# Four quadrants of the matrix array for row turning, decode products and 64-row sums, with ScalarE moving the second head pair back

## The chip, the cores and the metric

The kernel runs on one core of one Trainium2 chip. The metric is the device time of one execution in microseconds (us); less is better. Five engines work beside each other, each in the order of its own instruction list, and wait for each other by semaphores: TensorE (PE, and PEld for its loads of weights), VectorE (DVE), ScalarE (ACT), GpSimd (POOL) and SyncE (SP, which issues most DMAs).

## The reference

One inference step of a two-layer decoder. Each layer is a feed-forward block, a mixing block and another feed-forward block, all with residual adds. The mixing block projects the normed input once and splits the columns into four groups of heads: RWKV-7, RG-LRU, gated delta net (GDN) and gated linear attention (GLA).

```
x = x + 0.5 * _swiglu(_rmsnorm(x, norm_ffn1), ffn1_gate, ffn1_up, ffn1_down)
proj = _rmsnorm(x, norm_mix) @ w_in
o_rw, o_rg, o_gdn, o_gla = (the four groups, each 256 wide)
x = x + concatenate([o_rw, o_rg, o_gdn, o_gla]) @ w_out
x = x + 0.5 * _swiglu(_rmsnorm(x, norm_ffn2), ffn2_gate, ffn2_up, ffn2_down)
```

There are 256 prompt tokens of one sequence, worked in chunks of 64, and 8 x 8 decode tokens with given states: 320 tokens in all. Three groups have 4 heads of 64 values. In RWKV-7 and GDN the keys are scaled by the root of a sum of squares over the 64 rows of a head, and each decode sequence is multiplied with its own 64x64 state per head:

```
kk = _l2norm(_heads(k * rwkv_k_k, 64))            # x * rsqrt(sum(x*x) + 1e-12)
q = _l2norm(_heads(q, 64)) * 64 ** -0.5;  k = _l2norm(_heads(k, 64))
v_new = U - W @ S;  o = (q * eG) @ S + attn @ v_new
```

## The kernel before

Activations lie transposed: features on the 128 partitions, the 320 tokens (five chunks of 64, the fifth is the decode tokens) along the free axis. Four heads of 64 rows make two pairs p = 0, 1; within a pair head b = 0 is on partitions 0 to 63 and head b = 1 on 64 to 127 (`half[b]`). All operands with small matrices are of that form, so a product of one head has its operand on rows `half[b]` and its result, before the change, also on PSUM partitions `half[b]`: of the array's four 64x64 quadrants (row half, column half) only the two on the diagonal work.

Large products come from weight tiles of 128 x 1024. SP loads a tile (`raw`), ScalarE makes its high part (`split_hi`, L1124, 128x1024), VectorE the low part (`split_lo`, L1501), and TensorE multiplies in three terms (`three`, L477 to L479). A ring of four slots carries the tiles; ScalarE may write the high part of a unit only when the unit four before is used. From the fourteenth input tile on (`LATE`) only two places of `raw` are free, so a load waits until VectorE has made the low part of the unit two before.

In the mixing block the order of every engine is written out by hand. TensorE runs the 26 tiles of the input projection (each 24 matmuls of 128x320) and between them the small work: `lora`, `rw_sums` after tile 5, `rw_products` inside tile 9, `rw_rows` after tile 10, the steps of two 64x64 triangular inverses (`inverse_t` L774 and `inverse_y` L792, for g = 0 RWKV and g = 1 GDN), `gdn_sums` after tile 15, `gdn_products` (L631) after tile 19, `gdn_rows`, `gla_values`, and `decode_products` (L808) after tile 22 and in tile 23. Inverse steps already use all four quadrants: `inverse_unit(p, c, half[b ^ p])`. The same matmul in fp32 shows as two instructions in the trace. VectorE reads each tile out of PSUM (`evac`, L1572, L1573, L1582), which frees the bank for the tile after next, and does most of the elementwise work. ScalarE turns PSUM results into SBUF operands:

- `rw_rows`, `gdn_rows` and `gla_values` turn keys and values from columns to rows by a product with the identity (`to_rows`, L651); ScalarE copies each result (10 blocks of 64 columns, 128x640) out by one activation (L1285, L1287, L1289, L1348, L1350, L1356).
- `rw_sums` (L619) and `gdn_sums` (L666) sum squares over 64 rows with the 128x128 block-diagonal matrix of ones (`hones`); ScalarE takes Ln of each 128x320 result (L1268, L1319), then Exp.
- `decode_products(g)` writes 256 columns of bank 6 + g; ScalarE copies them out by one activation (`decode_out`, L1233). The stage after that needs them is `rg_gate`, which reuses the banks.
- `across` (L1219, L1220: two 64-partition copies that swap the halves) and `inverse_t` (L1211) on ScalarE serve the inverses. `gla_scale` (L1333, L1335) serves GLA.

Of the kernel before, what the change touches and what calls it, by code (L numbers as in the profile page):

```python
# [16 lines left out]
ACT = mybir.ActivationFunctionType  # L17
# [3 lines left out]
TOK = SEQ + DECB * DECT  # L21
GW, HD, NH, DK = 256, 64, 4, 32
CH = 64
# [101 lines left out]
    "hcen": 1, "yo": 1, "ysq0": 1, "ysq1": 1, "ysq2": 1, "cent_mm": 1, "cent_read": 1, "yrs": 3, "var_mm": 3, "VM": 4, "dec_mm": 3,  # L125
    "dec_decay": 3, "var_read": 3, "dec_add": 5, "sq_sum": 3,
}
V_STEPS, A_STEPS, G_STEPS = 102, 40, 14 + 3 * 6


class Signal:
# [43 lines left out]
def program(nc, xT, wts, par, cst, sin, mst, yT, sout, mout):  # L175
    with ExitStack() as ctx:
# [32 lines left out]
        ps = ctx.enter_context(nc.psum_tensor("ps", [128, 8, 512], F32))  # L209

        def A(u, n, pat=None, **kw):
            v = ar[:, u * TOK:u * TOK + n]
            return v.rearrange(pat, **kw) if pat else v
# [4 lines left out]
        def C(name, i=0, n=None):  # L218
            at, w = CST[name]
            return cs[:, at + i:at + i + (w if n is None else n)]  # L220
# [7 lines left out]
        rVt, kLt, bLt = (A(u, 640, CP, c=NC, p=2) for u in (18, 20, 22))  # L228
        gz, eG, kbe, qe = (A(u, 640, PT, p=2) for u in (24, 26, 28, 30))
        KQ = A(32, 1280, "q (c p k t) -> q c p k t", c=NC, p=2, k=2)  # L230
        bvt, gkdt = (A(u, 640, CP, c=NC, p=2) for u in (36, 38))
# [9 lines left out]
        ra, rsq, rtm = (A(u, 640, PT, p=2) for u in (47, 49, 40))  # L241
        gcp = A(73, 6 * CVP, PT, p=6)
        cq = A(52, 6 * TOK, PT, p=6)
        gsq = A(60, 4 * TOK, PT, p=4)
# [6 lines left out]
        lVt = A(75, 640, CP, c=NC, p=2)  # L251
# [23 lines left out]
        dec_out = [A(u, 256, "q (k p t) -> q k p t", k=2, p=2) for u in (42, 72)]  # L275
        nsq = A(49, 8 * TOK, PT, p=8)

        def mstate(name, p=2):
            at, n = MST[name]
            return ms[:, at:at + n].rearrange("q (p s v) -> q p s v", p=p, s=NSEQ)  # L280

        Mrw, Mgdn = mstate("rw"), mstate("gdn")
# [13 lines left out]
        half = [slice(0, 64), slice(64, 128)]  # L296
        I64 = [lev[half[b], 0, :] for b in range(2)]
# [29 lines left out]
        def banks(bank, runs, w=64):  # L327

            lo, hi = runs
            flat = ps[:, bank:bank + 3, :].rearrange("q b t -> q (b t)") if bank <= 5 else \  # L330
                ps[:, bank:8, :].rearrange("q b t -> q (b t)")
            return flat[:, lo * w:hi * w].rearrange("q (u t) -> q u t", u=hi - lo)
# [66 lines left out]
        def on(eng, layer, s, k=None):  # L399

            s = S[s] if isinstance(s, str) else s
            apart(eng, s, s.upto(layer, k)) if eng.engine in OWN_WAITS else eng.wait_ge(s.sem, s.upto(layer, k))
# [67 lines left out]
        def _(pe):  # L470
# [130 lines left out]
            def cht(v, c, p, b):  # L601
                return v[half[b], p, c * CH:(c + 1) * CH]


            def lora(layer):
                on(pe, layer, "lora_in")
                lo = P("lora", 0, 256)
                for rows, bank in ((slice(0, 32), 4), (slice(32, 64), 6), (slice(64, 128), 2)):
# [3 lines left out]
                        ins = pe.matmul(ps[:, bank + p, 0:TOK], lo[rows, p * 128:p * 128 + 128], xm[rows, 6, :], start=True, stop=True)  # L612
                    put(ins, "lora_mm")

            def rw_sums(layer):
                on(pe, layer, "sg")
                on(pe, layer, "kk_sq")
                for p in range(2):
                    ins = pe.matmul(ps[:, 4 + p, 0:TOK], C("hones"), rsq[:, p, :], start=True, stop=True)  # L619
                put(ins, "kk_sum")  # L620

            def rk_sums(layer):
# [24 lines left out]
            def to_rows(src, bank, name):  # L647

                def f(c, p, b):
                    u = c * 2 + p  # L650
                    return pe.matmul(ps[half[b], bank + u // 8, (u % 8) * 64:(u % 8) * 64 + 64], cht(src, c, p, b), I64[b],  # L651
                                     start=True, stop=True)
                put(each(f), name)

            def rw_rows(layer):
# [6 lines left out]
            def gdn_sums(layer):  # L662
                on(pe, layer, "gsq")
                on(pe, layer, "Gc")
                for k in range(4):
                    ins = pe.matmul(ps[:, 4 + k, 0:TOK], C("hones"), gsq[:, k, :], start=True, stop=True)  # L666
                put(ins, "gdn_sum")

            def gdn_decay(layer):
# [127 lines left out]
            def decode_products(layer, g):  # L797

                if g == 0:
                    on(pe, layer, "v_rows")  # L800
                    apart(pe, state_in, layer * 32 + 32)
                out = ps[:, 6 + g, 0:256].rearrange("q (k p t) -> q k p t", k=2, p=2)
                for q in range(DECB):
                    t = slice(q * DECT, q * DECT + DECT)
                    for p in range(2):
                        for b in range(2):
                            rhs = kkr[half[b], DEC, p, :, t] if g == 0 else kbe_qe[half[b], :, p, SEQ:][:, :, t]
                            ins = pe.matmul(out[half[b], :, p, t], (Mrw, Mgdn)[g][half[b], p, 1 + q, :], rhs, start=True, stop=True)  # L808
                put(ins, "R0_mm")

            def recurrences(layer):
# [306 lines left out]
        def _(act):  # L1118
# [58 lines left out]
            for layer in range(DEPTH):  # L1177
                st = Steps(act, a_step, layer, plain)

                def say(ins, name):  # L1180
                    return st(ins, S[name])
# [44 lines left out]
                def eye(g):  # L1226
                    if g == 0:
                        act.wait_ge(lo_ready.sem, layer * UNITS + IN0 + LATE)
                    say(act.activation(Y[g], lev[:, 0, :].unsqueeze(1).broadcast_to([128, 10, CH]), ACT.Copy), f"eye{g}")

                def decode_out(g):
                    on(act, layer, "R0_mm", g + 1)
                    say(act.activation(A(42 if g == 0 else 72, 256), ps[:, 6 + g, 0:256], ACT.Copy), "R0T")  # L1233

                ahead(1, 2)
                act.preload_act_table_set("sigmoid_and_others")
# [27 lines left out]
                act.wait_ge(S["prev"].sem, S["prev"].upto(layer))  # L1264
                say(act.activation(Pprev[:], sg[:], ACT.Exp, scale=-WDEC), "rw_P")
                act.wait_ge(S["kk_sum"].sem, S["kk_sum"].upto(layer))
                for p in range(2):
                    st(act.activation(rsq[:, p, :], ps[:, 4 + p, 0:TOK], ACT.Ln, bias=C("e12")))  # L1268
                st.settle()
                say(act.activation(rsq[:], rsq[:], ACT.Exp, scale=-0.5), "kk_rn")  # L1270
                on(act, layer, "gla_z")
                say(act.activation(ltm, ps[:, 6, 0:TOK], ACT.Abs, bias=P("gb")), "gla_ab")
# [9 lines left out]
                ahead(7, 8, 9)  # L1282
                eye(0)
                on(act, layer, "rw_rows_mm", 1)
                st(act.activation(rVt[:].rearrange("q c p t -> q (c p) t"), banks(2, (0, 10)), ACT.Copy))  # L1285
                on(act, layer, "rw_rows_mm", 2)
                st(act.activation(kLt[:].rearrange("q c p t -> q (c p) t"), banks(4, (0, 10)), ACT.Copy))  # L1287
                on(act, layer, "rw_rows_mm", 3)
                say(act.activation(bLt[:].rearrange("q c p t -> q (c p) t"), banks(6, (0, 10)), ACT.Copy), "rw_rows")  # L1289
                ahead(10, 11)  # L1290
                across(0, 1)
                inverse_t(0, 1)
# [22 lines left out]
                across(0, 3)  # L1315
                inverse_t(0, 3)
                act.wait_ge(S["gdn_sum"].sem, S["gdn_sum"].upto(layer))
                for k in range(4):
                    st(act.activation(gsq[:, k, :], ps[:, 4 + k, 0:TOK], ACT.Ln, bias=C("e12")))  # L1319
                st.settle()  # L1320
                say(act.activation(gsq[:], gsq[:], ACT.Exp, scale=-0.5), "gdn_rn")
                act.preload_act_table_set("exp_and_others")
                eye(1)
# [21 lines left out]
                inverse_t(0, 5)  # L1345
                ahead(20)
                on(act, layer, "gdn_rows_mm", 1)
                st(act.activation(bvt[:].rearrange("q c p t -> q (c p) t"), banks(4, (0, 10)), ACT.Copy))  # L1348
                on(act, layer, "gdn_rows_mm", 2)
                say(act.activation(gkdt[:].rearrange("q c p t -> q (c p) t"), banks(6, (0, 10)), ACT.Copy), "gdn_rows")  # L1350
                across(1, 1)
                inverse_t(1, 1)
                gla_scale(1)
                ahead(21)
                on(act, layer, "v_rows_mm")
                say(act.activation(lVt[:].rearrange("q c p t -> q (c p) t"), banks(6, (0, 10)), ACT.Copy), "v_rows")  # L1356
                gla_scale(2)
                across(1, 2)
                inverse_t(1, 2)
# [1073 lines left out]
```

## Time and profile before

| | |
|---|---|
| median of 3 runs | 1389.3 us (1388.21 to 1390.75) |
| the profiled execution's own time | 1388.47 us |
| its span in the trace | 1386.7 us |
| TensorE busy | 1353.0 us, 98% |
| VectorE busy | 862.9 us, 62% |
| ScalarE busy | 691.4 us, 50% |
| GpSimd busy | 75.4 us, 5% |
| mean granted TensorE clock | 0.997 |

Busy shares are means over stages with different limits. In the feed-forward stages TensorE streams without a pause. The two mixing blocks (about 254 to 435 us and 938 to 1119 us) are the only places that the change touches. A matmul is pipelined: its duration is longer than its distance to the next one, so rates are read from the length of a row that merges many.

### The profile page before, as it was taken

What the parts mean: (1) busy time and instruction counts of PE and PEld (TensorE: products, weight loads), DVE (VectorE), ACT (ScalarE), POOL (GpSimd) and SP (SyncE); (2) the same over time, 40 slices, a digit from 0 to 9 for tenths busy, and PEclk for the clock granted to TensorE, in tenths of its full rate; (3) what the DMA queues carried; (4) which work ended last, traced back from release to release, by engine and by line L of the source; (5) the groups of instructions that cost most, each with busy time, mean ns of one, the idle gap of its engine ahead of it and who ended that gap; (6) DMA issues with size and microseconds to landing.
All of it is one profiled execution on the core that took longest, in us unless ns stands there. A gap on an engine that the chain in (4) does not pass through costs nothing. (4 is left out here: it accounts for less than half of the span.)

```text
span 1386.7 us, 31381 instructions
## 1 busy us (share of the span) xinstructions
PE 1353.0 (98%) x12556; PEld 1308.9 (94%) x12556; DVE 862.9 (62%) x1329; ACT 691.4 (50%) x970; POOL 75.4 (5%) x109
## 2 busy tenths in 40 slices
PE   7999999999999999999999999999999999999997
PEld 7999999988888999999999999998888899999997
DVE  6656533897777765553475565358977767566433
ACT  7454433846455745443374453347455556454422
POOL 0000000200030100000010000010001301000000
PEclk9999999999999999999999999999999999999999
DMA  8544444313212544444454444433232135444441
GB/s 297 167 151 149 146 144 151 117 55 106 78 49 92 187 161 151 151 151 141 149 188 146 151 150 152 151 122 107 78 95 77 63 129 165 149 151 148 148 148 48
DMA packets 50765, 185.85 MB, mean 134 GB/s; under 512 B 5760, under 2 KB 6272, under 8 KB 50176
## 3 DMA queue, kind: packets, MB, share of 16 engines
q1 hardware_dynamic: 49104, 177.37, 39.4%
q10 hardware_dynamic: 1584, 7.35, 1.5%
q8 instruction: 60, 0.98, 0.3%
q14 instruction: 17, 0.14, 0.0%
HBM read 180.14 MB, written 4.56 MB: 133 GB/s over the span
## 5 line engine op out<-in xcount | busy, mean ns | idle before, releaser
L477 PE MATMUL ps<-xh,wh 128*128 128x320 f32 x1952 | 613.7, 314 | 12.7 <-DVE xl L1523 7.4
L1501 DVE TENSOR_TENSOR wl<-raw,wh 128x1024 fp32r<-128x1024 f32 x332 | 407.0, 1227 | 337.6 <-ACT wh L1124 337.2
L479 PE MATMUL ps<-xh,wl 128*128 128x320 f32 x1952 | 604.2, 310 | 0.0
L478 PE MATMUL ps<-xl,wh 128*128 128x320 f32 x1952 | 604.1, 310 | 0.0
L1124 ACT ACTIVATE wh<-raw 128x1024 fp32r<-128x1024 f32 x332 | 348.6, 1053 | 382.5 <-PE ps L479 371.5
L477 PEld LDWEIGHTS ps<-xh,wh 128*128 128x128 f32 x1952 | 367.5, 188 | 24.5 <-DVE wl L1501 7.8
L478 PEld LDWEIGHTS ps<-xl,wh 128*128 128x128 f32 x1952 | 367.7, 188 | 0.8
L479 PEld LDWEIGHTS ps<-xh,wl 128*128 128x128 f32 x1952 | 367.5, 188 | 0.0
L477 PE MATMUL ps<-hid_h,wh 128*128 (+1 forms) x704 | 217.9, 310 | 2.1 <-DVE hid_l L1548 2.1
L479 PE MATMUL ps<-hid_h,wl 128*128 (+1 forms) x704 | 217.5, 309 | 0.0
L478 PE MATMUL ps<-hid_l,wh 128*128 (+1 forms) x704 | 217.5, 309 | 0.0
L1165 ACT ACTIVATE gus<-gus 128x320 f32<-128x320 f32 x88 | 41.7, 473 | 189.7 <-DVE gus L1540 189.7
L477 PEld LDWEIGHTS ps<-hid_h,wh 128*128 128x128 f32 x704 | 132.1, 188 | 3.1 <-issue 3.1
L478 PEld LDWEIGHTS ps<-hid_l,wh 128*128 128x128 f32 x704 | 132.2, 188 | 0.0
L479 PEld LDWEIGHTS ps<-hid_h,wl 128*128 128x128 f32 x704 | 132.2, 188 | 0.0
L1540 DVE TENSOR_TENSOR gus<-ps,rstd 128x320 f32<-128x320 f32 x88 | 43.2, 491 | 101.4 <-PE ps L479 89.9
L2189 POOL TENSOR_TENSOR ar<-ar 128x320 f32<-128x320 f32 x35 | 31.7, 907 | 777.5 <-ACT ar L1147 773.4
L1165 ACT ACT_TABLE_LOAD x44 | 56.5, 1283 | 0.9
L1544 DVE TENSOR_TENSOR gus<-gus 128x320 f32<-128x320 f32 x88 | 43.4, 494 | 14.6 <-ACT gus L1165 2.6
L1548 DVE TENSOR_TENSOR hid_l<-gus,hid_h 128x320 f32 x88 | 42.6, 484 | 0.0
L1541 DVE TENSOR_TENSOR gus<-ps,rstd 128x320 f32<-128x320 f32 x88 | 42.3, 481 | 0.0
L1523 DVE SCALAR_TENSOR_TENSOR xl<-x,pr,xh 128x320 fp32r<-128x320 f32 x48 | 41.4, 898 | 0.1
(293 smaller groups left out, 974.5 us busy)
## 6 DMA issues: line engine op xcount, KB each, us to landing
raw<-wts SPq DMA_DIRECT2D x332, 512.0 KB, 3.5
ms<-mst ACTq DMA_DIRECT2D x2, 1440.0 KB, 9.2
mout<-ms ACTq DMA_DIRECT2D x2, 1440.0 KB, 7.2
x<-xT SPq DMA_DIRECT2D x4, 320.0 KB, 5.3
yT<-x SPq DMA_DIRECT2D x4, 320.0 KB, 2.2
cs<-cst SPq DMA_DIRECT2D x1, 652.0 KB, 9.0
pr<-par ACTq DMA_DIRECT2D x1, 429.0 KB, 4.1
pr<-par ACTq DMA_DIRECT2D x1, 425.0 KB, 5.2
```

The source lines that it names most:

```text
L477: pe.matmul(out, a, rh, start=start, stop=False)
L478: pe.matmul(out, a, rl, start=False, stop=False)
L479: return pe.matmul(out, b, rh, start=False, stop=stop)
L1124: act.activation(wh[:, s, :], raw_of(layer, n), ACT.Copy).then_inc(hi_ready.sem, 1)
L1165: act.activation(gus[:, m, :], gus[:, m, :], ACT.Silu).then_inc(sil_ready.sem, 1)
L1501: tt(wl[:, s, :], raw_of(layer, n), wh[:, s, :].bitcast(F32), ALU.subtract).then_inc(lo_ready.sem, 1)
L1523: stt(xl[:, k, :], x[:, k, :], P(name, k), xh[:, k, :].bitcast(F32), ALU.mult, ALU.subtract).then_inc(xl_ready.sem, 1)
L1540: tt(gus[:, m, :], ps[:, 2 * m, 0:TOK], rstd[:], ALU.mult).then_inc(gs_ready.sem, 1)
L1541: tt(gus[:, 2 + m, :], ps[:, 2 * m + 1, 0:TOK], rstd[:], ALU.mult).then_inc(gu_read.sem, 1)
L1544: tt(gus[:, m, :], gus[:, m, :], gus[:, 2 + m, :], ALU.mult).then_inc(act_ready.sem, 1)
L1548: tt(hid_l[:, at, :].rearrange("q a t -> q (a t)"), gus[:, m, :], hid_h[:, at, :].rearrange("q a t -> q (a t)").bitcast(F32), ALU.subtract ...
L2189: ins = gp.tensor_tensor(nsq[:, 0, :], nsq[:, 0, :], nsq[:, k, :], ALU.add)
```

## The change

Four things change, all in the mixing block.

1. `to_rows`: pair p = 1 writes to the opposite half (`half[b ^ p]`), each pair into a bank of its own (`bank + p`, 320 columns). The quadrants come in the order (0,0), (1,1), (0,1), (1,0). The number of matmuls is the same.
2. `rw_sums` and `gdn_sums`: each 128x128 product with the block-diagonal ones becomes two 64x64 products (`ones64`), for odd k in the crossed quadrants.
3. `decode_products`: pair 1 goes to the opposite half; both calls now use columns 0 to 127 of banks 6 and 7, so the second call first waits for ScalarE's copy of the first (`R0T`, 1).
4. ScalarE: what was one copy is now `home`: one activation of 128 partitions for pair 0, and two of 64 partitions that swap the halves for pair 1. `log_sums` does the same with Ln: one activation for even k, two for odd k. In all 19 more activations in each layer.

```diff
-V_STEPS, A_STEPS, G_STEPS = 102, 40, 14 + 3 * 6
+V_STEPS, A_STEPS, G_STEPS = 102, 59, 14 + 3 * 6
...
+            def ones64(b):
+                return C("hones")[half[b], 64 * b:64 * b + 64]
...
                 for p in range(2):
-                    ins = pe.matmul(ps[:, 4 + p, 0:TOK], C("hones"), rsq[:, p, :], start=True, stop=True)
+                    for b in range(2):
+                        ins = pe.matmul(ps[half[b ^ p], 4 + p, 0:TOK], ones64(b), rsq[half[b], p, :], start=True, stop=True)
...
                 def f(c, p, b):
-                    u = c * 2 + p
-                    return pe.matmul(ps[half[b], bank + u // 8, (u % 8) * 64:(u % 8) * 64 + 64], cht(src, c, p, b), I64[b],
-                                     start=True, stop=True)
+                    return pe.matmul(ps[half[b ^ p], bank + p, c * CH:c * CH + CH], cht(src, c, p, b), I64[b], start=True, stop=True)
...
                 for k in range(4):
-                    ins = pe.matmul(ps[:, 4 + k, 0:TOK], C("hones"), gsq[:, k, :], start=True, stop=True)
+                    for b in range(2):
+                        ins = pe.matmul(ps[half[b ^ k % 2], 4 + k, 0:TOK], ones64(b), gsq[half[b], k, :], start=True, stop=True)
...
+                else:
+                    on(pe, layer, "R0T", 1)
-                out = ps[:, 6 + g, 0:256].rearrange("q (k p t) -> q k p t", k=2, p=2)
+                out = ps[:, 6:8, 0:128].rearrange("q p (k t) -> q p k t", k=2)
...
-                            ins = pe.matmul(out[half[b], :, p, t], (Mrw, Mgdn)[g][half[b], p, 1 + q, :], rhs, start=True, stop=True)
+                            ins = pe.matmul(out[half[b ^ p], p, :, t], (Mrw, Mgdn)[g][half[b], p, 1 + q, :], rhs, start=True, stop=True)
...
+                def pieces(p):
+
+                    return ((half[0], half[1]), (half[1], half[0])) if p else ((slice(0, 128), slice(0, 128)),)
+
+                def home(dst, bank, name=None):
+
+                    for p in range(2):
+                        for to, at in pieces(p):
+                            d, n = dst[to, :, p, :], dst.shape[1]
+                            ins = act.activation(d, ps[at, bank + p, 0:n * CH].rearrange("q (c t) -> q c t", c=n), ACT.Copy)
+                            say(ins, name) if name and to is half[1] else st(ins)
+
+                def log_sums(dst, n):
+
+                    for k in range(n):
+                        for to, at in pieces(k % 2):
+                            st(act.activation(dst[to, k, :], ps[at, 4 + k, 0:TOK], ACT.Ln, bias=C("e12")[to]))
+                    st.settle()
...
-                    say(act.activation(A(42 if g == 0 else 72, 256), ps[:, 6 + g, 0:256], ACT.Copy), "R0T")
+                    home(dec_out[g], 6, "R0T")
...
-                for p in range(2):
-                    st(act.activation(rsq[:, p, :], ps[:, 4 + p, 0:TOK], ACT.Ln, bias=C("e12")))
-                st.settle()
+                log_sums(rsq, 2)
...
-                st(act.activation(rVt[:].rearrange("q c p t -> q (c p) t"), banks(2, (0, 10)), ACT.Copy))
+                home(rVt, 2)
...
-                for k in range(4):
-                    st(act.activation(gsq[:, k, :], ps[:, 4 + k, 0:TOK], ACT.Ln, bias=C("e12")))
-                st.settle()
+                log_sums(gsq, 4)
...
-                say(act.activation(lVt[:].rearrange("q c p t -> q (c p) t"), banks(6, (0, 10)), ACT.Copy), "v_rows")
+                home(lVt, 6, "v_rows")
```

ScalarE's list in the first layer, from the last inverse copy before GDN's sums (`raw<-ps`) through Ln, Exp, the table load and the identity copy to the high parts of the two next weight tiles. Before:

```order
145 L1211 ACTIVATE raw<-ps 128x2x16x8 [waits inv_mm0]
146 L1319 ACTIVATE ar<-ps,cs 128x320 [waits head_sums]
147 L1319 ACTIVATE ar<-ps,cs 128x320 x3
148 L1321 ACTIVATE ar<-ar 128x1280 [waits a_step]
149 L1322 ACT_TABLE_LOAD
150 L1229 ACTIVATE ar<-cs 128x640
151 L1124 ACTIVATE wh<-raw 128x1024 [waits unit_used,raw_in0]
```

And after the change (line numbers are those of the changed kernel):

```order
148 L1216 ACTIVATE raw<-ps 128x2x16x8 [waits inv_mm0]
149 L1252 ACTIVATE ar<-ps,cs 128x320 [waits head_sums]
150 L1252 ACTIVATE ar<-ps,cs 64x320 x2
151 L1252 ACTIVATE ar<-ps,cs 128x320
152 L1252 ACTIVATE ar<-ps,cs 64x320 x2
153 L1341 ACTIVATE ar<-ar 128x1280 [waits a_step]
154 L1342 ACT_TABLE_LOAD
155 L1234 ACTIVATE ar<-cs 128x640
156 L1129 ACTIVATE wh<-raw 128x1024 [waits unit_used,raw_in0]
```

Four Ln activations have become six; nothing else moved. The second place on ScalarE is the copy of GLA's values, between a weight tile's high part and the scale of GLA's second level, ahead of the inverse copy (`chain<-ps`) for which TensorE waits. Before:

```order
168 L1124 ACTIVATE wh<-raw 128x1024 [waits unit_used,raw_in1]
169 L1356 ACTIVATE ar<-ps 128x640 [waits v_rows_mm]
170 L1333 ACTIVATE ar<-ar 128x320 [waits lD]
171 L1335 ACTIVATE ar<-ar 128x320 [waits a_step]
172 L1219 ACTIVATE ar<-ar 64x320 [waits XY1]
173 L1220 ACTIVATE ar<-ar 64x320
174 L1211 ACTIVATE chain<-ps 128x80x4 [waits inv_mm1]
```

After:

```order
175 L1129 ACTIVATE wh<-raw 128x1024 [waits unit_used,raw_in1]
176 L1245 ACTIVATE ar<-ps 128x5x64 [waits v_rows_mm]
177 L1245 ACTIVATE ar<-ps 64x5x64 x2
178 L1353 ACTIVATE ar<-ar 128x320 [waits lD]
179 L1355 ACTIVATE ar<-ar 128x320 [waits a_step]
180 L1224 ACTIVATE ar<-ar 64x320 [waits XY1]
181 L1225 ACTIVATE ar<-ar 64x320
182 L1216 ACTIVATE chain<-ps 128x80x4 [waits inv_mm1]
```

One copy has become three. On TensorE the order stays as it was; in the decode products of the second group (g = 1, between the inverse step and GLA's first level) one wait is new. Before:

```order
1017 L774 MATMUL ps<-chain,ar 64x64 [waits XY1]
1018 L774 MATMUL ps<-chain,ar 64x64 x15
1019 L808 MATMUL ps<-ar,ms 64x2x8 x32
1020 L724 MATMUL ps<-ar 64x64 [waits gdn_rows]
1021 L724 MATMUL ps<-ar 64x64 x19
```

After:

```order
1017 L777 MATMUL ps<-chain,ar 64x64 [waits XY1]
1018 L777 MATMUL ps<-chain,ar 64x64 x15
1019 L813 MATMUL ps<-ar,ms 64x2x8 [waits R0T]
1020 L813 MATMUL ps<-ar,ms 64x2x8 x31
1021 L727 MATMUL ps<-ar 64x64 [waits gdn_rows]
1022 L727 MATMUL ps<-ar 64x64 x19
```

## Rows read from the trace of the kernel before

**Rows 1.** The page's first part: busy time by engine.

```profile
PE 1353.0 (98%) x12556; PEld 1308.9 (94%) x12556; DVE 862.9 (62%) x1329; ACT 691.4 (50%) x970; POOL 75.4 (5%) x109
```

**Rows 2.** Busy time in stretches; columns: length, then engines, clock, DMA share, GB/s.

```profile
295.00:330.00 35.00, 33.03 (x472) 29.79 (x470) 32.78 (x62) 18.08 (x26) 1.47 (x2) 0.95 0.25 77
...
349.00:370.00 21.00, 20.68 (x448) 19.07 (x445) 20.52 (x41) 10.87 (x21) 2.99 (x5) 1.00 0.27 87
370.00:377.00 7.00, 7.00 (x176) 6.59 (x176) 2.14 (x3) 2.66 (x5) 0.00 (x0) 1.00 0.26 84
```

**Rows 3.** TensorE in order of time, 295 to 373 us: start, length, count.

```profile
295.28 3.71 PE L651 MATMUL ps<-cs,ar 64*64 64x64 f32 x120
...
302.64 0.81 PE L774 MATMUL ps<-raw,ar 64*64 64x64 f32 x40
...
327.82 2.42 PE L666 MATMUL ps<-ar,cs 128*128 128x320 f32 x8
...
370.80 2.04 PE L808 MATMUL ps<-ar,ms 64*64 64x16 f32 x64
```

**Rows 4.** What TensorE waited for, 255 to 430 us: total, times, longest.

```profile
PE ps L477 <- DVE ar L1573: 1.6, 1, 1.6
PE ps L690 <- DVE ar L1641: 1.1, 1, 1.1
PE ps L774 <- DVE raw L1879: 0.7, 1, 0.7
...
PE ps L631 <- DVE ar L1720: 0.5, 1, 0.5
```

**Rows 5.** TensorE in the second layer, after tile 16.

```profile
1017.14 0.27 PE L792 MATMUL ps<-raw 64*64 64x64 f32 x2 [1.30 <-ACT raw L1211]
```

**Rows 6.** ScalarE in order of time, 328 to 345 us; in brackets the idle time before.

```profile
328.98 0.63 ACT L1223 ACTIVATE ar<-ar 128x512 f32<-128x512 f32 x1 [0.56 <-DVE ar L1658]
...
333.29 0.36 ACT L1211 ACTIVATE raw<-ps 128x256 f32<-128x256 f32 x1
333.67 1.78 ACT L1319 ACTIVATE ar<-ps,cs 128x320 f32<-128x320 f32 x4
...
338.72 1.99 ACT L1124 ACTIVATE wh<-raw 128x1024 fp32r<-128x1024 f32 x2
...
344.53 1.06 ACT L1124 ACTIVATE wh<-raw 128x1024 fp32r<-128x1024 f32 x1 [0.41 <-DMA raw<-wts]
```

**Rows 7.** VectorE in order of time, 339 to 348 us.

```profile
339.79 1.23 DVE L1501 TENSOR_TENSOR wl<-raw,wh 128x1024 fp32r<-128x1024 f32 x1 [4.08 <-ACT wh L1124]
...
345.62 1.22 DVE L1501 TENSOR_TENSOR wl<-raw,wh 128x1024 fp32r<-128x1024 f32 x1 [1.13 <-ACT wh L1124]
...
347.56 0.81 DVE L1720 TENSOR_TENSOR ar<-ar,ps 128x640 f32<-128x640 f32 x1
```

**Rows 8.** ScalarE's copies: a pair of 128x320 out of PSUM, and the crossing pieces.

```profile
309.51 0.74 ACT L1295 ACTIVATE ar<-ps 128x320 f32<-128x320 f32 x2
...
359.33 0.47 ACT L1219 ACTIVATE ar<-ar 64x320 f32<-64x320 f32 x1
359.83 0.47 ACT L1220 ACTIVATE ar<-ar 64x320 f32<-64x320 f32 x1
360.20 0.68 ACT L1211 ACTIVATE chain<-ps 128x640 f32<-128x640 f32 x1
```

**Rows 9.** ScalarE, 365 to 368 us.

```profile
365.15 0.70 ACT L1356 ACTIVATE ar<-ps 128x640 f32<-128x640 f32 x1
365.76 0.47 ACT L1333 ACTIVATE ar<-ar 128x320 f32<-128x320 f32 x1
...
367.63 0.41 ACT L1211 ACTIVATE chain<-ps 128x320 f32<-128x320 f32 x1
```

**Rows 10.** TensorE at the inverse step after tile 22's first half.

```profile
368.10 0.40 PE L792 MATMUL ps<-ar,chain 64*64 64x64 f32 x12 [0.32 <-ACT chain L1211]
```

**Rows 11.** The same six microseconds in layer one and layer two.

```profile
316.00:322.00 6.00, 5.17 (x40) 5.19 (x41) 5.72 (x11) 5.07 (x7) 1.47 (x2) 0.72 0.35 97
1000.00:1006.00 6.00, 5.57 (x87) 5.32 (x88) 5.68 (x12) 4.92 (x7) 1.47 (x2) 1.00 0.35 113
```

More of the change, by code:

```diff
@@ L1284, in _ @@
                 on(act, layer, "rw_rows_mm", 1)
-                st(act.activation(rVt[:].rearrange("q c p t -> q (c p) t"), banks(2, (0, 10)), ACT.Copy))
+                home(rVt, 2)
                 on(act, layer, "rw_rows_mm", 2)
-                st(act.activation(kLt[:].rearrange("q c p t -> q (c p) t"), banks(4, (0, 10)), ACT.Copy))
+                home(kLt, 4)
                 on(act, layer, "rw_rows_mm", 3)
-                say(act.activation(bLt[:].rearrange("q c p t -> q (c p) t"), banks(6, (0, 10)), ACT.Copy), "rw_rows")
+                home(bLt, 6, "rw_rows")
                 ahead(10, 11)
@@ L1347, in _ @@
                 on(act, layer, "gdn_rows_mm", 1)
-                st(act.activation(bvt[:].rearrange("q c p t -> q (c p) t"), banks(4, (0, 10)), ACT.Copy))
+                home(bvt, 4)
                 on(act, layer, "gdn_rows_mm", 2)
-                say(act.activation(gkdt[:].rearrange("q c p t -> q (c p) t"), banks(6, (0, 10)), ACT.Copy), "gdn_rows")
+                home(gkdt, 6, "gdn_rows")
                 across(1, 1)
```

## The prediction

> **What bounds the kernel now.** I read the busy shares first. TensorE is busy for 98% of the span [rows 1], which invites the conclusion that every nanosecond taken from it is gained. The windows of the mixing block correct that: from 295 to 330 us TensorE is busy for 33.0 of 35 us, but VectorE for 32.8 of 35 as well, and from 349 to 370 the two have 20.7 and 20.5 of 21. Only from 370 on is TensorE alone full (7.0 of 7 us, VectorE 2.1) [rows 2]. So in most of the stretch two engines run neck and neck, and the waits must say who leads. TensorE's waits are small but they lie all along: for VectorE's evacuation ahead of tile 9 (1.6 us), its transpose (0.7) and its bonus product (1.1) at 314 to 317 us, and its value product (0.5) ahead of L631 [rows 4]. In layer two it also waits 1.30 us for ScalarE's inverse copy after tile 16 [rows 5]. Wherever such a wait stands, time that TensorE saved ahead of it only makes the wait longer. I therefore go from one of these meeting points to the next and ask at each whether the engine that TensorE meets has moved.
>
> **The rates.** An inverse step in all four quadrants takes 0.81 us for 40 instructions; take off 0.22 for the tail of the last one, and it is 15.1 ns from one to the next. Row turning on the diagonal takes 3.71 us for 120, which is 29.3 ns, and the decode products 2.04 us for 64, 29.0 ns [rows 3]. If the other two quadrants work as they do in the inverse step, one turn of 40 instructions falls by 39 x 14.2 ns = 0.55 us, a decode call by 63 x 13.9 ns = 0.88 us. The wide sums take 2.42 us for 8 instructions, 0.284 us each after the tail [rows 3]; four quadrants need half the time, so GDN's sums save 1.14 us and RWKV's, half as many, 0.57.
>
> TensorE thus saves per layer: 6 turns x 0.55 = 3.3, two decode calls 1.76, sums 1.71, together 6.8 us. What of it is on the path?
>
> **To tile 9.** RWKV's sums (0.57) are followed by the 1.6 us wait for VectorE [rows 4], whose work up to there needs nothing from the sums until ScalarE's Exp, and that has 2 us to spare. Gain 0. ScalarE's third Ln (below, 0.5 us) fits into the same room. Cost 0.
>
> **Row turning of RWKV to tile 16.** Three turns save 1.7 us at 297 us. The following inverse step needs ScalarE's halves swap, which waits for VectorE's GLA decay; VectorE has no idle time between 297 and 332 us in its timeline. The waits of 0.7 and 1.1 us at 314 to 317 us are for VectorE too [rows 4]. Gain 0. ScalarE's three copies become nine, some 1.8 us more; it ends near 300.3 instead of 299.7, and TensorE needs them only after tile 11, at 301. Cost 0.
>
> **GDN's sums, where the change costs.** They save 1.14 us at 330 us, but the next thing after tile 16 is an inverse step that starts at 333.70, right after ScalarE's copy ended at 333.65; that copy hangs on a chain which VectorE's convolution released at 328.98 [rows 6]. In layer two TensorE waits 1.30 us there already [rows 5]. Gain 0. Then ScalarE is the leader: Ln from 333.67, Exp, a table load, the identity, and the high part of a weight tile at 338.72 [rows 6], for which VectorE has idled 4.08 us; its low part lets the DMA for the unit two on start, the next high part waits 0.41 us for that DMA, VectorE 1.13 us for this high part, and then come the products that end with L1720, for which TensorE waits 0.5 us [rows 4, 6, 7]. There is no slack in this chain. Two more Ln at (1.78 - 0.55) / 3 = 0.41 us each are 0.82 us. A crossing piece is followed by the next after 0.50 us instead of the 0.37 us of a plain piece [rows 8], which happens twice: 0.26 more. Bounds 0.8 and 1.2; I take 1.0, since the rows for crossing pieces read SBUF and not PSUM. The lower end below that is nothing, if pieces of 64 partitions overlap; I keep 0 for a rival. So L631 starts 1.0 us later.
>
> The Trainium skill, TensorEngine Tiling (Array Packing), "PSUM Bottleneck", says that packing the array speeds up TensorE but not the way out of PSUM, which may then become the limit. The rows above bear that out for ScalarE here; by it the sign of this step is a loss, which the sum already has.
>
> **GDN's turns and GLA's.** TensorE would save 1.1 us in GDN's two turns, but ScalarE takes the weight tile's high part after tile 20 before it can copy, so it starts no earlier; six pieces at 0.37 to 0.50 us instead of two copies (0.61 us from one start to the next [rows 9]) end about 1.3 us late, the inverse step follows 1.3 late. VectorE, already 1.0 late from above and without a gap, hides the rest. GLA's turn saves 0.55 into that same lateness. Its copy stands 0.61 us ahead of the next activation [rows 9]; three pieces at 0.37 + 0.50 + 0.37 = 1.24 us [rows 8] are 0.63 more (bounds 0.5 and 0.9), and the inverse copy at 367.63 comes directly behind it. TensorE waits 0.32 us for exactly this copy [rows 10]. So the inverse step at 368.10 starts 1.0 + 0.6 = 1.6 us late. Every turn's gain is gone.
>
> **Decode.** From 370 to 377 us TensorE has no idle time [rows 2], so the two calls count in full: minus 1.76 us. The new wait for R0T hides behind tile 23's first half (2.0 us) and an inverse step (0.7): ScalarE has been waiting for the products and needs some 0.6 us for three pieces of 128 columns. Behind the waiting instruction are GLA's first level and half a tile; if the cover were gone the wait would cost 0.6.
>
> **Sum.** Per layer +1.0 +0.6 -1.76 = -0.16 us, both layers -0.3 us. The profiled execution took 1388.47 us for a span of 1386.7; -0.3 gives 1388.2. The median of the runs is 0.8 above that execution, so on it I forecast 1389.0 us. With the bounds of the two ScalarE terms (0.8 to 1.2, 0.5 to 0.9) the forecast alone reaches from -0.9 to +0.7 us, and with the spread of the three runs from 1387.5 to 1390.5.
>
> **Rivals.**
> - TensorE alone decides. Then all 6.8 us per layer count and the time is 1375.7. For it speaks the 98%; against it every wait in rows 4 and 5. Chance 0.04.
> - ScalarE's pieces cost nothing at its two tight places, for instance because 64-partition pieces overlap. Then only the decode gain is left: -3.5 us, 1385.8. With some of the turns' gain 1384. Against it: the crossing pieces now take 0.50 us [rows 8]. Chance 0.15.
> - The decode products gain nothing, and the kernel gets slower. Their instructions of 16 columns go at 29.0 ns like those of 64 columns [rows 3], so streaming does not set their pace; if it is something that both column halves share, such as the loading of weights through a row half, four quadrants bring nothing. It decides as soon as a call keeps more than 1.9 of its 2.04 us. Then +1.6 per layer stays: +3.2, 1392.5. Against it: the inverse step loads a new weight for every instruction too and goes at 15.1 ns. Chance 0.10.
> - The clock falls. From 316 to 322 us it is 0.72 of full (in part at the lower of its two levels, 1.2 GHz), behind TensorE's waits of 0.7 and 1.1 us; at the same place in layer two it stays 1.00 [rows 11]. That cost 0.28 x 6 = 1.7 us, unseen since VectorE led. The change adds idle time of 1 to 2.5 us ahead of three meeting points. A fall between 349 and 370 us would hit where little slack is: up to 1.7 us per layer, 1392.4. Chance 0.07.
>
> The skill's same page, "Gotcha 1: PSUM Pressure", says that different row tiles cannot use one PSUM bank at the same time. Here two row halves write one bank both before and after, and the inverse step does so at 15.1 ns. If the rule governed, the decode products would gain nothing, which is the third rival; the trace disagrees.
>
> **How the numbers follow.** The forecast has 0.64. What a measurement of this kernel can tell from no change is about 0.2%, 2.8 us. Faster than that: the first two rivals, 0.19. Slower: most of the last two, just beyond the bound, 0.16. The rest, 0.65, is the same. The range holds 8 in 10 from 1385.2, which takes in most of the second rival, to 1392.2.
>
> **What would show it.** L774-like rates in the new turns and decode calls (0.81 and about 1.16 us); TensorE waiting longer for VectorE at 314 to 317 us, about 1.1 us more after tile 16, and over 1 us ahead of L631; six Ln in 2.6 to 3.0 us; L631 about 1.0 us later than now after the common start of the layer; the inverse step of rows 10 about 1.6 us late; the start of GLA's first level within 0.5 us of where it was. Wrong would be a shortened stretch between tile 9 and L631, or a decode call that is still near 2 us.

## The result and the profile after

The change made the kernel slightly slower: 1391.49 us median of 20 runs against 1389.03, ratio 1.0016 with a 95% interval of 1.0009 to 1.0023. One execution of each kernel took 4.6 ms; the ratio leaves these two out. The forecast was 1389.0 us and no change. The time lies inside the range of 1385.2 to 1392.2, and 2.5 us is within the 0.2% that the text called the same, but the loss is clear of the interval and the sign of the forecast sum (-0.3 us) was wrong. The profiled execution took 1391.6 us for a span of 1389.8.

The busy line answers [rows 1]: TensorE has 9 us less to do and the kernel is later.

```profile
PE 1343.9 (97%) x12580; PEld 1298.3 (93%) x12580; DVE 862.1 (62%) x1329; ACT 703.6 (51%) x1008; POOL 75.3 (5%) x109
```

TensorE in order of time, first layer (start, length, count, idle before and who ended it). These answer [rows 3, 5, 10].

```profile
294.88 1.98 PE L654 MATMUL ps<-cs,ar 64*64 64x64 f32 x120
309.29 0.27 PE L795 MATMUL ps<-raw 64*64 64x64 f32 x2 [1.54 <-ACT raw L1216]
327.35 1.26 PE L669 MATMUL ps<-ar,cs 64*64 64x320 f32 x16
333.33 0.27 PE L795 MATMUL ps<-raw 64*64 64x64 f32 x2 [1.00 <-ACT raw L1216]
349.59 2.40 PE L635 MATMUL ps<-ar 64*64 64x128 f32 x40 [1.91 <-DVE ar L1740]
362.42 0.80 PE L795 MATMUL ps<-ar,chain 64*64 64x64 f32 x38 [1.40 <-ACT chain L1216]
369.94 0.81 PE L795 MATMUL ps<-ar,chain 64*64 64x64 f32 x40 [1.07 <-ACT chain L1216]
372.63 1.12 PE L813 MATMUL ps<-ar,ms 64*64 64x16 f32 x64
```

The three RWKV turns take 1.98 us instead of 3.71, GDN's sums 1.26 instead of 2.42, a decode call 1.12 instead of 2.04: the quadrants do what they should. The saved time went into waits: new ones of 1.54 us where the row is at 309 and of 1.00 us after tile 16, 1.91 us at L635 (it was 0.5 in [rows 4]), 1.40 and 1.07 at the inverse steps (the latter 0.32 in [rows 10]). The waits for VectorE ahead of tile 9 and at 314 to 317 us stayed at 1.6, 0.7 and 1.1 us. The prediction had looked for longer waits at 314 to 317 us; what the RWKV turns saved went into the wait for ScalarE's inverse copy at 309 instead.

ScalarE in the two tight places, and the first three Ln one by one; these answer [rows 6, 9].

```profile
333.30 3.28 ACT L1252 ACTIVATE ar<-ps,cs 128x320 f32<-128x320 f32 x6
...
333.30 0.53 ACT L1252 ACTIVATE ar<-ps,cs 128x320 f32<-128x320 f32 x1
333.85 0.53 ACT L1252 ACTIVATE ar<-ps,cs 64x320 f32<-64x320 f32 x1
334.41 0.52 ACT L1252 ACTIVATE ar<-ps,cs 64x320 f32<-64x320 f32 x1
...
339.84 1.99 ACT L1129 ACTIVATE wh<-raw 128x1024 fp32r<-128x1024 f32 x2
...
366.25 1.33 ACT L1245 ACTIVATE ar<-ps 128x320 f32<-128x320 f32 x3
367.60 0.47 ACT L1353 ACTIVATE ar<-ar 128x320 f32<-128x320 f32 x1
...
369.47 0.41 ACT L1216 ACTIVATE chain<-ps 128x320 f32<-128x320 f32 x1
```

The Ln group takes 3.28 us instead of 1.78: +1.50. A Ln of 64 partitions lasts as long as one of 128 (0.53 us), and none starts before the one ahead of it has ended (0.55 us from start to start), while the four of before overlapped (0.41). GLA's copy takes 1.35 us up to the next activation instead of 0.61: +0.74.

The path through both mixing blocks, measured from the layer's first LoRA product (261.80 and 945.39 us before, 261.38 and 945.53 after; worked out from the rows of both traces):

| us from the layer's first LoRA product | layer 1 before | after | layer 2 before | after |
|---|---|---|---|---|
| L631 (after: L635) starts | 86.72 | 88.21 | 86.58 | 89.79 |
| inverse step of [rows 10] starts | 106.30 | 108.56 | 106.15 | 110.13 |
| first decode call starts | 109.00 | 111.25 | 108.84 | 112.82 |
| GLA's first level starts | 115.37 | 115.78 | 115.21 | 117.35 |
| head centering (L992, L997) starts | 162.20 | 162.77 | 161.61 | 164.61 |

From the end of the first block to the start of the second, and behind the second, nothing differs by more than 0.1 us. The sum is 0.57 + 3.00 = 3.6 us, less 0.4 that this execution began its first layer earlier: 3.1 us, the difference of the spans. Up to GLA's first level, layer one is as the forecast had it but for sizes. Two more things come in, both larger in layer two. One is TensorE's clock (windows of the changed kernel; the column before the last two is the granted clock):

```profile
316.00:322.00 6.00, 5.55 (x43) 5.57 (x44) 5.68 (x12) 4.26 (x6) 1.47 (x2) 0.72 0.34 111
1000.00:1008.00 8.00, 7.43 (x48) 7.26 (x48) 6.19 (x12) 4.58 (x6) 1.47 (x2) 0.57 0.39 132
```

In layer one the clock falls as before [rows 11], 0.28 x 6 = 1.7 us of full speed, and VectorE hides it. In layer two it falls for twice that, 0.43 x 8 = 3.4 us, where before it stayed at 1.00. Tile 14 then ends so late that VectorE has to wait for it, and L635 comes 3.2 instead of 1.5 us late:

```profile
1008.08 0.49 DVE L1600 SCALAR_TENSOR_TENSOR ar<-ps,rstd 128x320 f32<-128x320 f32 x1 [1.57 <-PE ps L479]
```

The other is a stop in the recurrences, of which the profile shows no cause:

```profile
1094.36 0.21 PE L824 MATMUL ps<-ar 64*64 64x64 f32 x1 [0.67 <-issue]
```

In all it is 1.0 us in two stops in this kernel (0.31 us in layer one, 0.67 in layer two), and none in the kernel before. So the 3.6 us of the profiled execution are 0.8 from the sizes on the path, 1.7 from the long fall and 1.0 from the stops.

How often the long fall comes can be read from the mean granted clock of every execution. Seven of the 19 executions of the changed kernel read 0.995 or less, and they took 1391.4 to 1393.7 us; the other twelve took 1390.0 to 1391.9 with a median of 1390.8, 0.6 below the median of all 19. Of the 79 executions of the kernel before that were timed beside the experiments, five read 0.995 (1390.1 to 1391.2 us) and none less; from 0.996 to 0.999 a lower reading did not go with a longer time. So the long fall adds some 0.6 us to the median of the changed kernel; this is an estimate, since only the profiled executions show where the clock fell.

### The profile page after: what moved, and what is told of

It reads as the page before. It is cut to its first block and busy times, and to the rows that moved or that the text cites. A ratio compares the mean times of both kernels' runs of the same rounds, so it can differ in the third digit from the quotient of the medians.

```text
span 1389.8 us, 31467 instructions
## 1 busy us (share of the span) xinstructions
PE 1343.9 (97%) x12580; PEld 1298.3 (93%) x12580; DVE 862.1 (62%) x1329; ACT 703.6 (51%) x1008; POOL 75.3 (5%) x109
```

## The experiments

All are timed beside the kernel before, whose median in the three batches was 1388.93, 1389.3 and 1389.2 us; each ratio is to its own batch. The two kernels with the identity later have five executions each, GDN's sums alone nine, the others eleven. GLA's first level is read from one profiled execution, in us after the layer's first LoRA product; that product itself starts between 261.4 and 262.6 us in the thirteen profiled executions, so medians less than about 1 us apart say little about the mixing blocks. Theory 1: ScalarE's pieces do not overlap, and their two tight places (+1.5, +0.7 us per layer) outweigh the two decode calls (-1.84). Theory 2: falls of the clock make the loss. Theory 3: the stops come from where the instruction stream stands (in the first expectation "theory 3" is the third rival of the prediction).

| kernel | median us | ratio to before, 95% | GLA's first level, layer 1 / 2 |
|---|---|---|---|
| before | 1389.0 | 1 | 115.37 / 115.21 |
| the change | 1391.5 | 1.0016 (1.0009 to 1.0023) | 115.78 / 117.35 |
| decode alone | 1385.2 | 0.9975 (0.9966 to 0.9984) | 113.41 / 113.32 |
| GDN's sums alone | 1392.7 | 1.0025 (1.0015 to 1.0035) | 116.92 / 118.40 |
| turns alone | 1390.6 | 1.0010 (1.0001 to 1.0019) | 116.07 / 115.97 |
| change, GDN's sums as before | 1386.5 | 0.9983 (0.9974 to 0.9992) | 114.19 / 114.27 |
| change, turns and sums uncrossed | 1390.9 | 1.0015 (1.0006 to 1.0024) | 115.95 / 117.58 |
| change, filled after tile 13 | 1391.0 | 1.0017 (1.0007 to 1.0026) | 115.55 / 115.58 |
| change, all longer waits filled | 1390.5 | 1.0009 (1.0000 to 1.0018) | 115.59 / 115.63 |
| before, filled after tile 13 | 1389.0 | 0.9998 (0.9989 to 1.0007) | 115.13 / 115.20 |
| GDN's sums as before, 8 instructions more | 1387.7 | 0.9990 (0.9981 to 0.9999) | 114.37 / 114.40 |
| decode, identity later | 1384.5 | 0.9963 (0.9950 to 0.9977) | 112.84 / 114.58 |
| decode, identity later, filled | 1383.9 | 0.9961 (0.9948 to 0.9975) | 112.81 / 112.82 |

**Decode alone.** The kernel before with only the two edits in `decode_products` and `home` in `decode_out`.

> The kernel before with the decode products alone changed (four quadrants, one copy into three pieces). Theory 1 (what decides is ScalarE: its pieces do not overlap each other, each costs its full duration, which makes the two tight ScalarE places 1.5 and 0.7 us later per layer, against 1.84 us that the two decode calls give per layer): both tight places are untouched, so the gain stands alone, 2 x 1.84 = 3.7 us below before, ratio 0.9973, and the first level of GLA starts about 1.8 us earlier in each layer. Theory 2 (the loss of the full change comes from TensorE's clock, which falls at tile 14 after more idle time): no idle time is added ahead of tile 14, so the clock is as before and the gain stands too. Theory 3 (the decode products gain nothing): ratio 1.000.

Measured 3.7 us below before, as theory 1 has it; the interval is 1.2 us to either side, so the match to the tenth is luck. The third rival, that 16-column products gain nothing, is out:

```profile
370.69 1.12 PE L810 MATMUL ps<-ar,ms 64*64 64x16 f32 x64
```

**GDN's sums, taken out and put in alone.** In the changed kernel:

```diff
                 for k in range(4):
-                    for b in range(2):
-                        ins = pe.matmul(ps[half[b ^ k % 2], 4 + k, 0:TOK], ones64(b), gsq[half[b], k, :], start=True, stop=True)
+                    ins = pe.matmul(ps[:, 4 + k, 0:TOK], C("hones"), gsq[:, k, :], start=True, stop=True)
...
-                log_sums(gsq, 4)
+                for k in range(4):
+                    st(act.activation(gsq[:, k, :], ps[:, 4 + k, 0:TOK], ACT.Ln, bias=C("e12")))
+                st.settle()
```

> The changed kernel, but with GDN's sums and their Ln as before (four 128x128 products, four Ln of 128 partitions). Theory 1: ScalarE's chain ahead of L631 is 1.5 us shorter in each layer, nothing else moves, so about 3.0 us below the changed kernel, near 1388.3 us, ratio to before 0.9995. Theory 2: the sums stand behind tile 14, so the clock falls as often as in the changed kernel and the time stays near 1391 us. If TensorE's time in the sums counted, the kernel would be up to 2.2 us slower than theory 1 says.

> The kernel before with GDN's sums alone changed (eight 64x64 products, six Ln). Theory 1 (ScalarE's pieces do not overlap; its chain ahead of L631 decides): the six Ln take 3.28 us instead of 1.78, L631 starts 1.50 us later in each layer and all behind it as well, 3.0 us above before, ratio 1.0022. Theory 3 (TensorE stalls with nothing to wait for in the recurrences, 0.3 us in layer one and 0.7 in layer two, in every kernel that has the sums' 8 more instructions per layer, and in none without them): up to 1.0 us on top, 1393. Rival (the sums' 1.14 us on TensorE counts): about 0.7 us above before.

Taken out, the kernel is 5.0 us below the full change, not 3.0; put in alone, it is 3.4 us above before. The sign and the place are theory 1's. The surplus is what theory 1 leaves out: no stop in the recurrences (1.0 us) and no long fall in the profile of the first. Its clock does fall at tile 14 of layer two, to 0.72 from 1000 to 1006 us, but a fall of that length stays hidden: GLA's first level comes at 114.19 and 114.27. In the second kernel the clock of layer two falls behind a wait of 2.11 us ahead of L631, where nothing hides it. The 40 products take 2.40 us in layer one and 3.97 in layer two:

```profile
349.84 2.40 PE L631 MATMUL ps<-ar 64*64 64x128 f32 x40 [2.00 <-DVE ar L1730]
...
1034.78 3.97 PE L631 MATMUL ps<-ar 64*64 64x128 f32 x40 [2.11 <-DVE ar L1730]
```

```profile
1032.00:1038.00 6.00, 3.89 (x35) 3.66 (x35) 5.97 (x12) 1.06 (x1) 0.00 (x0) 0.72 0.32 98
```

From L631 to the next inverse step of the second group takes 14.07 us in layer two instead of 12.52 in layer one: 1.55 us. The fourth rival had put up to 1.7 on such a fall.

**Turns alone.** The kernel before with the edits in `to_rows` and `home` for its six copies.

> The kernel before with row turning alone changed (six calls in four quadrants, six copies into eighteen pieces). Theory 1: nothing moves up to GDN's turns; there VectorE is not late as in the changed kernel, the copy of GLA's values takes 1.35 us up to the next activation instead of 0.61, and the inverse step behind it starts 0.7 us later: +0.7 per layer, 1.5 us above before, ratio 1.001; no stall of TensorE in the recurrences. Rival (what TensorE saves in the turns counts): up to 6.6 us below before. Theory 2 (the clock): the three RWKV turns leave TensorE 1.5 us more idle after tile 12, so the long fall at tile 14 in layer two comes here too and adds up to 1.6 us more.

Measured 1.3 us above before, ratio 1.0010. Three microseconds less of TensorE in each layer bring no gain, and GLA's first level comes 0.7 and 0.76 us later. The long fall of theory 2 did not come in the profiled execution (clock 1.00 from 1000 to 1006 us), though TensorE was as idle ahead of it as in the full change (waits of 1.54, 0.70 and 1.12 us).

The three parts timed alone add up to -3.7 + 3.4 + 1.3 = +1.0 us, while the full change has +2.5. RWKV's sums were never timed alone, and stops and long falls differ from kernel to kernel; what makes up the difference is not shown.

**Turns and sums back on the diagonal, same pieces.** Besides the lines shown, both kinds of sums write to `half[b]`.

```diff
-                    return pe.matmul(ps[half[b ^ p], bank + p, c * CH:c * CH + CH], cht(src, c, p, b), I64[b], start=True, stop=True)
+                    return pe.matmul(ps[half[b], bank + p, c * CH:c * CH + CH], cht(src, c, p, b), I64[b], start=True, stop=True)
...
+                    if not cross:
+                        return ((half[0], half[0]), (half[1], half[1])) if p else ((slice(0, 128), slice(0, 128)),)
```

> The changed kernel, but row turning and both kinds of sums stay on the diagonal of the array, and ScalarE copies in the same three pieces without swapping the halves; the decode products stay as changed. This takes away everything that TensorE gains outside decode and keeps the number of ScalarE's pieces. Theory 1: same time as the changed kernel within 0.5 us, since TensorE only waits less at tile 9, after tile 12, after tile 16 and at L631. If TensorE's own time decided, up to 2 x 5.0 = 10 us more. If it is the crossing of halves, not the number of pieces, that costs ScalarE its overlap, the six Ln take 2.6 us instead of 3.28 and the kernel is some 1 to 2 us faster than the changed one.

The turns are back at their old length, and the kernel takes the same time as the full change within the intervals, where 10 us more were due if TensorE's time decided. Its gain outside decode is worth nearly nothing, but two small things cancel. L635 starts 0.32 and 0.27 us earlier than in the full change, since the Ln are shorter (below). GLA's first level starts 0.17 and 0.23 us later all the same: between the two, the slower turns of GDN and GLA cost 0.5 us per layer. ScalarE now waits for GLA's turn (last row), so "every turn's gain is gone" holds only to half a microsecond. ScalarE's six Ln:

```profile
295.17 3.71 PE L654 MATMUL ps<-cs,ar 64*64 64x64 f32 x120
```

```profile
333.55 3.00 ACT L1254 ACTIVATE ar<-ps,cs 128x320 f32<-128x320 f32 x6
...
333.55 0.94 ACT L1254 ACTIVATE ar<-ps,cs 128x320 f32<-128x320 f32 x2
...
334.52 0.52 ACT L1254 ACTIVATE ar<-ps,cs 64x320 f32<-64x320 f32 x1
...
366.72 1.21 ACT L1247 ACTIVATE ar<-ps 128x320 f32<-128x320 f32 x3 [0.20 <-PE ps L654]
```

Uncrossed they take 3.00 us, crossed 3.28. Of the 1.50 us, 1.22 come from splitting and 0.28 from swapping halves. The expected 2.6 us was wrong: the first two together end at 334.49, so they still overlap, but the third, a piece on the other half, starts only at 334.52. Neighbours on different halves do not overlap even without a swap.

**Filled waits.** Products of constants into a bank that nobody reads at that time, ahead of TensorE's waits.

```diff
+            def filler(layer, n):
+                on(pe, layer, "Gb")
+                for _ in range(n):
+                    pe.matmul(ps[:, 6, 0:256], C("ones"), C("tri"), start=True, stop=True)
...
-13: lambda l: (inverse_t(l, 0, 2), gdn_base(l))
+13: lambda l: (filler(l, 1), inverse_t(l, 0, 2), filler(l, 2), gdn_base(l))
```

> The changed kernel with products of constants put on TensorE ahead of its two waits after tile 13 (one of 256 columns ahead of the inverse step, two ahead of gdn_base; their result is not used). They fill idle time of 0.7 and 1.1 us per layer. Theory 1: the clock no longer falls or falls less, but most of a fall is absorbed by the wait after tile 16, so between 0 and 1.7 us below the changed kernel, about 1390.5. Theory 2: the clock stays at 1.00 in both layers from 1000 to 1014 us too, and the time comes down by 2 us or more, to that of before (1389) or below.

> The kernel before with the same products of constants ahead of the two waits after tile 13. The clock does not fall between 316 and 322 us any more. Theory 1: that fall was hidden, the median stays within 0.5 us of before, and the runs above 1390 us with a clock of 0.995 become rarer. Theory 2: the fall cost its 1.5 us, so the time comes down by 1 us or more.

> The changed kernel with products of constants in all the waits that the change made longer: after tile 13, after tile 16, ahead of L631, and ahead of the two inverse steps of the second inverse. Theory 1 (of the loss, ScalarE's net is 0.3 us per layer, a stall of TensorE in the recurrences 1.0 us in all, the rest is falls of the clock): no fall of the clock in the mixing blocks any more; GLA's first level starts 0.3 us later than before in each layer; about 1390.3 us, 1.2 below the changed kernel's 1391.5. Rival (clock falls cost nothing in the median): as the changed kernel, 1391.5. Should the fillers themselves delay (they are no longer than the waits), up to 1 us more.

The first kept the clock at 1.00 in both layers where it had fallen, and the 1.7 us of layer two went (117.35 to 115.58). Yet its median is only 0.4 us below the change's and its ratio no lower (1.0017 to 1.0016). A fall came in layer one behind a wait of 2.4 us after tile 16 instead (0.57 from 334 to 338 us), but GLA's first level is not later for it (115.55). That execution reached its first LoRA product 1.2 us later than the changed kernel's; why the median kept its height is not shown. In the kernel before the fall was hidden: filled, its clock reads 0.999 in all eleven executions, and the median moves by 0.3 us. With all longer waits filled no fall is left in the mixing blocks of the profiled execution:

```profile
255.00:430.00 175.00, 164.33 (x2861) 143.92 (x2860) 141.74 (x286) 105.32 (x184) 20.78 (x34) 1.00 0.27 83
940.00:1115.00 175.00, 165.18 (x2870) 145.06 (x2869) 142.28 (x287) 106.51 (x186) 20.71 (x34) 1.00 0.26 83
```

The ratio goes from 1.0016 to 1.0009, 1.0 us less. The intervals overlap, so this is no better a measure of the clock's part of the median than the 0.6 us above. What is left above before in the profile is ScalarE's net (0.22 and 0.42 us at GLA's first level) and a stop of 0.9 us.

**Eight instructions more.** The kernel with plain GDN sums and four products of 16 columns in the wait ahead of L631.

> The kernel with GDN's sums as before and everything else changed, plus four products of 16 columns in TensorE's wait ahead of L631: it then has as many TensorE instructions ahead of the recurrences as the full change (8 more per layer). Theory 3 (the stall with nothing to wait for comes from where the instruction stream then stands): the stall of 0.3 us in layer one and 0.7 in layer two appears, about 1387.4 us. Otherwise (the stall has to do with how late ScalarE or VectorE are): no stall, 1386.5 us like the kernel without the four.

It is 1.2 us slower than without them (ratios 0.9990 and 0.9983, the intervals overlap). The four products themselves make GLA's first level 0.18 and 0.13 us later, and a stop appears, in layer two only:

```profile
PE ps L825 <- issue: 0.4, 1, 0.4
```

The expected pattern (0.3 and 0.7) did not come; stops of 0.2 to 0.9 us show in the traces of nine of the eleven experiments, but not in the kernel before, in its filled version, or in the one with plain GDN sums. Decode alone and the turns alone add no TensorE instruction and still have a stop of 0.2 and of 0.3 us, so "in none without them", written before GDN's sums alone, is wrong. More TensorE instructions ahead are therefore not needed for a stop; the cause stays open.

**ScalarE's chain shortened.** Decode alone, and one move:

```diff
-                eye(1)
                 ahead(16, 17)
+                eye(1)
```

> The kernel before with the decode products changed, and ScalarE's identity for the second inverse (0.64 us up to the next activation) moved from ahead of the high parts of two weight tiles to behind them. Theory 1: this is the chain that sets L631, so it starts 0.64 us earlier in each layer less the 0.46 us that TensorE waited at L631 being the room: TensorE arrives at 0.46 us before, so at most 0.46 us per layer is gained, 0.9 us below the kernel with the decode products alone, near 1384.3 us. Rival (ScalarE's chain does not decide): 1385.2 us, no change.

> The decode products changed, ScalarE's identity moved behind two weight tiles, and the two waits after tile 13 filled. Theory 1: the long fall of the clock at 1000 us, which took 1.7 us in the profile of the kernel without fillers, is gone; about 1383.7 us, ratio to before 0.996, and less spread. Rival: 1384.5 us, no change.

L631 starts 86.06 us after the layer's start instead of 86.62 with decode alone, GLA's first level 0.57 us earlier: in the trace the chain named in the prediction decides in this direction too. The medians (1385.2 and 1384.5) cannot confirm it, since the intervals overlap. In layer two the clock fell long, at 0.57, without any idle time added ahead of it, and L631 came 1.7 us later than in layer one (87.78). So the idle time that the full change adds is not needed for a long fall; whether it makes one likelier is open, though 7 of 19 executions against 5 of 79 speak for it:

```profile
998.00:1006.00 8.00, 7.53 (x48) 7.35 (x52) 6.09 (x12) 4.76 (x7) 1.46 (x2) 0.57 0.42 131
```

With the waits filled the same window reads 1.00, layer two is as layer one, and the kernel has the lowest median, 1383.9 us, 0.39% below before; its five executions lie within 0.8 us. From the one without fillers (ratio 0.9963 against 0.9961) the times do not tell it apart.

```profile
998.00:1006.00 8.00, 8.00 (x104) 7.72 (x105) 7.65 (x17) 5.07 (x6) 1.47 (x2) 1.00 0.44 133
```

## Why the prediction was wrong

- **Who leads at each meeting point**: right. Gains of the RWKV sums, all six turns and GDN's sums were put at 0; the uncrossed kernel and the turns alone show it, but for the 0.5 us per layer that the GDN and GLA turns are worth once ScalarE's chain is late. The longer waits for VectorE at 314 to 317 us did not come; the wait at 309 took their place, with the same gain of 0.
- **The step that failed is the Ln term**, "Two more Ln at (1.78 - 0.55) / 3 = 0.41 us each are 0.82 us ... I take 1.0", bounds 0.8 to 1.2. It measured 1.50, outside the bounds. The argument kept the overlap of the old Ln for the new ones and charged a lost overlap only between crossing pieces. The runs showed that splitting alone costs 1.22 us, as much as the upper bound, and swapping halves 0.28 more. The row to use was the full duration of one Ln: six without overlap are 6 x 0.55 = 3.3 us. As a bound it was in reach. The 0.37 us of a plain piece was misread too: it is half the length of a pair [rows 8], whose second copy starts 0.32 us after the first. With 0.32 the text's own sum for the Ln is 1.18, still short.
- **GLA's copy**: 0.63 predicted, 0.74 measured, inside its bounds; same reason.
- **Decode**: 0.88 per call predicted, 0.92 measured.
- **The sum** per layer was +1.0 + 0.6 - 1.76 = -0.16. With the measured sizes it is +1.50 + 0.74 - 1.84 = +0.40, and layer one shows +0.41. This alone turns the sign: +0.8 us.
- **The clock** stood as a rival with 0.07, priced 1.7 us per layer, at a place between 349 and 370 us. The price was right (1.7 in layer two here, 1.55 in GDN's sums alone), the place and the chance too narrow: it came at tile 14 for twice as long as before, where I had counted a fall as hidden. A fall as short as the one seen is hidden there (GDN's sums as before, layer two); the text did not weigh a longer one.
- **The stops** of 1.0 us were not in the text at all; no row of before shows one.

In the profiled execution these three, 0.8, 1.7 and 1.0, make up the 3.6 us. In the median the 0.8 rests on the experiments, the clock's part is estimated at 0.6 (1.0 by the filled kernel), and the stops were measured in single executions only; together they come near the 2.5 us, but this sum is not shown. The time lies in the stated range because the range was wide, not because the sum was right.

## What to carry to other kernels

Before an engine at 98% is relieved, list who ends each of its waits: here 5 of 6.8 us per layer were saved ahead of a wait for another engine and were worth nothing, or at most 0.5 in the last turns, while the one place without waits gave its full 1.84. When a copy or a Ln is cut into pieces by partitions, charge every piece its full duration: here it did not fall with the partitions (Ln 0.53 us for 128 and for 64), and neighbours on different halves did not overlap (0.55 us from start to start instead of 0.41). A part that gains and a part that loses should be timed alone: the decode products by themselves are 0.25% faster.

## What the runs showed of the hardware

- On ScalarE an activation of 64x320 out of PSUM lasts as long as one of 128x320 (copy 0.43 and 0.43 us, Ln 0.52 and 0.53). Neighbours of 128 partitions overlap by about 0.1 us (Ln 0.41 from start to start, copies 0.32), and so does a piece on the first half behind one of 128 (0.43). After any other change of the partition half they do not: 0.55 us from the first half to the second, and from the second to 128 partitions.
- Products of 16 columns gain from the four quadrants as those of 64 columns do: 64 of them in 1.12 us instead of 2.04, though 16 columns are little to stream.
- A fall of TensorE's clock took 1.7 or 3.4 us of full speed in these traces. It came behind idle time of 0.7 and 1.1 us, or of 2.1 and 2.4 us, in some executions and layers and not in others with the same idle time (the turns alone, layer two). Products of constants in the waits after tile 13 kept it from that place in the profiled executions of all four kernels that had them; the kernel with 8 instructions more had no fall there without them.
- TensorE stopped for 0.2 to 0.9 us in the recurrences with nothing to wait for in nine of the eleven experiments and in the changed kernel, not in the kernel before. No experiment shows why.
